# Five of the first eight modulation slabs summed on TensorE as rows instead of on VectorE as columns

## The reference, cut to what matters

```
mod = silu(c) @ ada_w + ada_b                 # c: 2048 values, ada_w: 2048 x 6144
shift, scale, gate = split(mod, 3)
h = rms_norm(x, norm_g) * (1 + scale) + shift
proj = h @ w_in                               # 2048 x 9296
```

## Time and profile before

| | us |
|---|---|
| median of 3 runs | 2428.26 (2428.01 to 2428.3) |
| the profiled execution: its time | 2428.43 |
| its span (first to last instruction) | 2426.6 |
| TensorE busy | 2384.8 (98%) |
| VectorE busy | 1973.3 (81%) |
| ScalarE busy | 1299.3 (54%) |
| GpSimd busy | 99.0 (4%) |
| HBM traffic | 212 GB/s over the span |

### The profile page before, as it was taken

One profiled execution on the slowest core, in us unless ns is written; L12 is line 12 of the kernel. 1 busy time (PEld: TensorE's weight loads), 2 busy tenths in 40 slices (PEclk: granted clock), 3 DMA queues, 4 the chain that ended last, 5 costly groups with the idle time before them and its releaser, 6 DMA issues.

```text
span 2426.6 us, 28811 instructions
## 1 busy us (share of the span) xinstructions
PE 2384.8 (98%) x11030; PEld 1979.5 (82%) x11030; DVE 1973.3 (81%) x2564; ACT 1299.3 (54%) x1703; POOL 99.0 (4%) x150
## 2 busy tenths in 40 slices
PE   5999999999999999999999999999999999999998
PEld 4888878888888888888888888888888888888887
DVE  6998988766889899897777768965699898988776
ACT  4757765445555555654444544554555555555443
POOL 0210000000000000000000212100000000000000
PEclk8999999999999999999999999999999999999999
DMA  9997665474566566566656655446666565565654
GB/s 383 360 385 246 240 208 171 166 262 167 192 208 208 191 208 196 186 199 215 229 188 205 196 196 193 160 142 203 218 210 200 188 212 188 195 222 189 224 191 156
DMA packets 190649, 515.46 MB, mean 212 GB/s; under 512 B 17920, under 2 KB 18208, under 8 KB 188208
## 3 DMA queue, kind: packets, MB, share of 16 engines
q1 hardware_dynamic: 178160, 465.31, 56.5%
q0 software_dynamic: 11824, 46.14, 5.1%
q10 hardware_dynamic: 528, 2.16, 0.2%
HBM read 507.26 MB, written 6.29 MB: 212 GB/s over the span
## 4 chain that ended last, share of the span: by engine, by line
PE 95%; DVE 2%; SPq 1%; DMA 0%; issue 0%; ACT 0%; DVEq 0%; ACTq 0%
PE acc L808 18%; PE acc L810 17%; PE acc L809 17%; PE acc L1276 4%; PE acc L1275 4%; PE acc L1277 4%; PE wk L1276 4%; PE wk L1275 4%; PE wk L1277 4%; PE acc L1317 1%; PE acc L1316 1%; PE acc L1318 1%; PE wk L1317 1%; PE wk L810 1%; PE wk L809 1%; PE wk L1316 1%
## 5 line engine op out<-in xcount | busy, mean ns | idle before, releaser
L2098 DVE TENSOR_TENSOR lo<-raw,hi 128x1024 fp32r<-128x1024 f32 (+2 forms) x428 | 486.8, 1188 | 110.2 <-ACT hi L1486 108.6
L1486 ACT ACTIVATE hi<-raw 128x1024 fp32r<-128x1024 f32 (+2 forms) x428 | 414.6, 1026 | 253.0 <-PE acc L810 122.1
L2100 DVE SCALAR_TENSOR_TENSOR lo<-raw,gcols,hi 128x1024 fp32r<-128x1024 f32 (+1 forms) x392 | 479.7, 1267 | 50.8 <-ACT hi L1486 48.3
L808 PE MATMUL acc<-hi,h 128*128 128x512 f32 x1312 | 519.4, 396 | 1.5 <-DVE lo L2098 0.5
L810 PE MATMUL acc<-hi,h 128*128 128x512 f32 x1312 | 511.7, 390 | 0.0
L809 PE MATMUL acc<-lo,h 128*128 128x512 f32 x1312 | 511.3, 390 | 0.0
L1486 ACT ACTIVATE hi<-raw,gcols 128x1024 fp32r<-128x1024 f32 (+1 forms) x392 | 416.6, 1124 | 140.4 <-PE acc L810 59.6
L808 PEld LDWEIGHTS acc<-hi,h 128*128 128x128 f32 x1312 | 246.8, 188 | 53.7 <-issue 2.7
L810 PEld LDWEIGHTS acc<-hi,h 128*128 128x128 f32 x1312 | 246.6, 188 | 52.3
L809 PEld LDWEIGHTS acc<-lo,h 128*128 128x128 f32 x1312 | 246.9, 188 | 49.1
L808 PE MATMUL acc<-hi,g_hi 128*128 128x512 f32 x544 | 211.9, 390 | 0.0
(11 more groups left out here) (445 smaller groups left out, 3403.8 us busy)
## 6 DMA issues: line engine op xcount, KB each, us to landing
raw<-in_w_ffn_gate SPq DMA_DIRECT2D x176, 512.0 KB, 3.8
raw<-in_w_ffn_up SPq DMA_DIRECT2D x176, 512.0 KB, 4.7
raw<-in_w_ffn_down SPq DMA_DIRECT2D x176, 512.0 KB, 4.7
raw<-in_w_in SPq DMA_DIRECT2D x144, 512.0 KB, 4.8
raw<-in_w_kv SPq DMA_DIRECT2D x64, 512.0 KB, 4.9
ada_raw<-in_ada_w POOLq DMA_DIRECT2D x38, 512.0 KB, 7.2
gate_raw<-in_ada_w POOLq DMA_DIRECT2D x32, 512.0 KB, 6.2
raw<-in_w_out SPq DMA_DIRECT2D x32, 512.0 KB, 4.8
```

Source lines behind the costliest of these rows:

```text
L808: pe.matmul(o, l_hi, w_hi[:, c], start=first, stop=False, skip_group_check=loaded)
L1486: ins = act.activation(hi[:, m % HI_SLOTS, c], raw[:, r, c], ACT.Copy, scale=scale)
L2098: ins = vec.tensor_tensor(lo[:, r, c], raw[:, r, c], hi[:, m % HI_SLOTS, c], ALU.subtract)
L2100: ins = vec.scalar_tensor_tensor(out=lo[:, r, c], in0=raw[:, r, c], scalar=gcols[:, st.gain, k:k + 1], in1=hi[:, m % HI_SLOTS, c], op0=ALU ...
```

## The change

Slabs 0, 1, 2, 3 and 5 are summed on TensorE, with the operands the other way round: a column of `silu(c)`, 128 partitions x 1, is stationary, and the slab is the moving operand, 512 columns at a time. Each slab takes four products of 128x512; all of them accumulate into one row of 2 x 512 sums in PSUM banks 2 and 3 (partition 0). ScalarE copies that row to SBUF (`ada_row`), and eight products with one row of 128 as stationary operand and a single 1.0 as moving one turn it into the eight PSUM columns, onto which `quarter_columns` adds what VectorE has summed. VectorE keeps slabs 4, 6 and 7 of the first eight. The transpose of the gains moves behind the first row sum; the row sum of slab 5 stands between `turn_xn` 1 and 2; the eight products stand between `turn_xn` 4 and 5; only `turn_xn` 6 and 7 are left behind `quarter_columns`. On SP the fetches of modulation slabs 11 and 12 move one `w_in` slab later, each with its wait.

```
-    PE_ADA = (1,)
+    PE_ADA = (0, 1, 2, 3, 5)
+    VEC_FIRST = (4, 8, 16, 24)
...
# SP
             if m == 3:
                 sp.wait_ge(xn_ready, 2)
                 ada_fetch(10, quarter_landed[2])
+            if m == 4:
                 sp.wait_ge(ada_added, added(7))
                 ada_fetch(11, early_landed[2])
-            if m == 4:
+            if m == 5:
                 sp.wait_ge(ada_added, added(8))
                 ada_fetch(12, early_landed[3])
...
# TensorE
-        pe.wait_ge(gains_in, 16 * 7)
-        pe.transpose(acc[:, 0, 0:P], rows[:], ident[:]).then_inc(rows_turned, 1)
...
+        def ada_row_sum(a):
+            ada_wait(pe, a)
+            for part in range(2):
+                for e in range(2):
+                    b = part * GW + e * HALF
+                    ins = pe.matmul(acc[0:1, 2 + e, :], c_col[:, 2 * a + part:2 * a + part + 1], ada_slot(a)[:, b:b + HALF],
+                                    start=a == PE_ADA[0] and part == 0, stop=a == PE_ADA[-1] and part == 1)
+            ins.then_inc(ada_taken, 1)
+
+        def row_into_columns():
+            pe.wait_ge(row_copied, 1)
+            pe.wait_ge(gains_out, 1)
+            for f in range(4):
+                for e in range(2):
+                    b = e * HALF + f * P
+                    pe.matmul(quarter_col(acc, e, f), ada_row[0:1, b:b + P], ones[0:1, 0:1], start=f % 2 == 0, stop=False,
+                              skip_group_check=True)
+
+        def turn_xn_when_parked(i):
+            if i >= 4:
+                pe.wait_ge(xn_parked, i - 3)
+            turn_xn(i).then_inc(turned, 1)
...
         pe.wait_ge(c_silu, 1)
+        ada_row_sum(0)
+        pe.wait_ge(gains_in, 16 * 7)
+        pe.transpose(acc[:, 0, 0:P], rows[:], ident[:]).then_inc(rows_turned, 1)
+        for a in (1, 2, 3):
+            ada_row_sum(a)
         pe.wait_ge(xn_ready, TT)
-        for i in range(4):
-            turn_xn(i).then_inc(turned, 1)
+        for i in range(2):
+            turn_xn_when_parked(i)
+        ada_row_sum(5)
+        for i in range(2, 5):
+            turn_xn_when_parked(i)
+        row_into_columns()
+        turn_xn_when_parked(5)
         quarter_columns(0, acc, False)
-        for i in range(4, 8):
-            pe.wait_ge(xn_parked, i - 3)
-            turn_xn(i).then_inc(turned, 1)
+        for i in range(6, 8):
+            turn_xn_when_parked(i)
...
# ScalarE
         conv_to(0)
-        for i in range(4):
+        for i in range(2):
+            park(i)
+        act.wait_ge(ada_taken, len(PE_ADA))
+        act.activation(ada_row[:].rearrange("p (e n) -> p e n", e=2), acc[0:1, 2:4, :], ACT.Copy).then_inc(row_copied, 1)
+        for i in range(2, 4):
             park(i)
...
# VectorE, in ada(a)
-                if k == 0 and a < N_MOD:
+                if kk == 0 and a in VEC_FIRST:
```

More of the change, by code:

```diff
@@ L156, in build @@
     ones_r = at("ones_r", [P, P], slot(1), F32R)
+    ada_row = at("ada_row", [1, GW], G0 + 79)
     ada_sum = [gate[:, 0:GW], gate[:, GW:D], tmp1, tmp2, gate[:, 0:GW], gate[:, GW:D]]
@@ L532, in build @@
     x_fetched = sem("x_fetched")
+    row_copied = sem("row_copied")
     own_landed = sem("own_landed")
@@ L945, in quarter_columns @@
                 ins.then_inc(ada_turned, 1)
-        pe.wait_ge(c_silu, 1)
[L948 to L957, removed]
```

## The result

| | before | after |
|---|---|---|
| median, us | 2428.3 (2427.85 to 2429.66, 9 runs) | 2433.28 (2431.42 to 2437.1, 9 runs) |
| ratio to before, 95% interval | | 1.002 (1.0011 to 1.0028) |
| span of the profiled execution, us | 2426.6 | 2431.5 |

The changed kernel is slower, by 5.0 us or 0.2%; the forecast was 3.4 us faster. The opening went as the prediction said or better. The loss is made 20 to 30 us behind it, in one wait and the slower clock that follows it.

A forecast was written before the change was run, and what follows sets the result against it. TensorE, busy 2384.8 of 2426.6 us, bounds the kernel; an earlier product start, worth 3.4 us by product 9, takes the profiled 2428.43 to 2425.0, or 2424.9 as median (that execution is 0.17 above it); range 2423.0 to 2429.0.

The forecast's parts named there:

- VectorE's sum 2.4 us earlier: Opening, VectorE: without slab 5, and with slab 6 waiting for its landing, its sum ends at 36.85 instead of 39.26.
- Row sums at 6.8 us for slab 0 and 3.5 to 3.7 from slab 1 on: Opening, TensorE: slab 0 summed at the lower clock, 1.2 GHz, later slabs at the upper, 2.4 GHz.
- never raised: Rival, opening: one-column row sums never raise TensorE's clock, everything behind is 11 to 12 us late; 2440, chance 0.12.
- TensorE late: Rival, opening: clock drops behind slab 5's sum, 2427.7; harder form, slab 5 itself at 1.2 GHz, 2430.9; chance 0.18.
- Eight small products done by 36.1, transpose 5 by 36.7: Opening, TensorE: both finish just before VectorE's sum; TensorE is free 0.15 us ahead of it.
- Columns at the lower level, start 3.7 us earlier: Opening: columns at 1.2 GHz, two transposes behind them instead of four; large products start at 42.3 instead of 46.05.
- all at the upper clock: Rival, opening: columns, transposes and first products also run at 2.4 GHz, products start at 41.3; 2423.8, chance 0.20.
- The first products gain what the start gains: Large products behind the opening: they keep the 3.7 us earlier start, with 2.3 us still at the lower clock.
- Scales of the second quarter at 85.5, product 9 gains 3.4: Second quarter: VectorE's tables end at 85.5 instead of 87.87, scales gain 3.5, product 9 behind them 3.4 us.
- The SP edit worth 0: SP's queue: moving modulation slabs 11 and 12 behind `w_in` 3 and 4 costs nothing, since VectorE adds them much later.
- For the landings of `w_in` behind the start I show no row; I take 0, with half a us of doubt: DMA landings of `w_in` after the products start: assumed to cost the earlier start 0, at most 0.5 us.
- nothing comes of it: Rival, 50 to 98 us: a `w_in` landing or ScalarE hand-over gives the gain back; 2428, chance 0.08.

The follow-up runs named there:

- e9: e2 with modulation slabs 16 and 17 also held on GpSimd until VectorE has summed slab 15: 2425.28 us, ratio 0.9987 to the kernel before.
- e5: The kernel before plus only the hold of two slab sums on GpSimd's slabs 13 to 15, no row sums: 2429.6 us, ratio 1.0006.
- e2: The changed kernel with GpSimd's fetches of slabs 13 to 15 waiting for two more VectorE slab sums: 2426.62 us, ratio 0.9992 to the kernel before.
- e3: The changed kernel with SP's order put back, slabs 11 and 12 not moved: 2433.36 us, ratio 1.002 to the kernel before.
- e1: The changed kernel with GpSimd's fetches of slabs 13 to 15 waiting for one more VectorE slab sum: 2429.57 us, ratio 1.0003 to the kernel before.
- e4: The changed kernel with ScalarE converting `w_in` slab 5 one product later, behind the bank hand-over: 2431.53 us, ratio 1.0013 to the kernel before.
- e6: The kernel before with only transposes 4 and 5 moved ahead of the columns, VectorE's sum untouched: 2427.75 us, ratio 0.9998.
- e10: e9 with GpSimd's small rows sent behind slab 14 instead of 15: 2429.17 us, ratio 1.0003 to the kernel before.

## Why the prediction was wrong, point by point

- **VectorE's sum 2.4 us earlier:** right. The columns started 39.31 - 36.93 = 2.4 earlier, behind `gate`.
- **Row sums at 6.8 us for slab 0 and 3.5 to 3.7 from slab 1 on:** right, 6.55 and 3.5 to 3.6. The rival *never raised* fell. *TensorE late* did not occur in this profile, but a part of its harder form did in e9, with the same opening: slab 5 took 5.29 instead of 3.59 (the rival had 6.8) and the columns started behind TensorE's own queue, at 38.18. So where the clock falls is in part luck of the execution, and that the forecast came close here is so too.
- **Eight small products done by 36.1, transpose 5 by 36.7:** right, 36.0 and 36.6.
- **Columns at the lower level, start 3.7 us earlier:** half right. The clock fell at 38.0, in the columns, so the first pair took 38.02 - 36.93 = 1.1 instead of 1.9 and the start gained 4.4. This is between the forecast and the rival *all at the upper clock*. The Trainium skill ("TensorE: Matmul & The Clock Gate", Part 4) says that transposes don't count as busy for the clock; here the clock fell 5.4 us behind the last row sum, over transposes and small products alike, so this trace does not tell the two apart. The opening of before speaks against the Trainium skill here. It has only the 16 transposes between 22.0 and 39.3 us; in e5, whose opening is the same, they took 3.54 us instead of 3.67, because the last ones ran faster, and the granted clock stayed at 1.00 behind them until 34.1. So there the clock rose over transposes alone; the difference is 0.13 us in one profile, and what makes it rise stays open.
- **The first products gain what the start gains:** 0.4 too much, since the lower level now reached 3.2 us into them.
- **Scales of the second quarter at 85.5, product 9 gains 3.4:** wrong for the changed kernel (93.83 and a loss of 4.8), right for the mechanism once the landing is in time: 85.31 in e2 and 86.47 in e9, and product 9 gains 2.7 and 2.6. The rest is the wait of product 8 in e2, 0.88, and the later start in e9.
- **The SP edit worth 0:** right in the time (e3, 2433.36 against 2433.28), but not because slab 12 is early enough: VectorE waited 3.48 us for it.
- **"For the landings of `w_in` behind the start I show no row; I take 0, with half a us of doubt":** this is the step that failed. The term is 6.9 us of wait and 1.8 of clock. I had costed the SP edit, but not the queue of GpSimd, which the change does not touch and whose fetches are released by VectorE, the engine that the change makes faster. The trace of before held it. `hi` 5 waited 2.97 us for its landing, the hand-over behind it began at 65.92 and its first bank was done at 66.5, and product 4 started at 69.00: 2.5 us of slack, less than the 3.7 by which I moved TensorE forward. With the start that came about, net 4.0 earlier (64.99), a delay of 1.6 us was due even at an unchanged landing (4.0 - 2.5, and 0.14 from the hand-over to the product); the later landing adds 5.4, and together they make the 7.0 by which product 4 missed its due start.
- **The rival *nothing comes of it*** named the place (a landing of `w_in`, or the hand-over on ScalarE) and had 0.08. Its price was wrong: it was capped at the gain. A delayed transfer is not bounded by the gain that set it off, and the clock adds to it. That is why the range ended 4.3 us short.
- **What the runs show and what stays open.** That GpSimd's earlier fetches cause the late landing, and with it most of the loss, is shown: landing and wait follow the hold (e1, e2), SP's order does not cause it (e3), ScalarE's order passes it on (e4), and moving TensorE without VectorE does not set it off (e6). The 1.6 us that were due without it are worked out from the rows, not run by themselves. e9 starts its products 3.3 us earlier than the kernel before, has 2.6 of it at product 9, 2.5 in the span and 3.0 in the median; what more slab 5 at the upper level would bring there was not separated. A split of the DMAs' time other than by the queues' turns was not tried.

## What to carry to other kernels

When a change makes an engine faster, list the transfers that this engine releases, on every queue, and ask whether the DMAs are full at that time; if they are, each of them moves ahead of something, and the slack of the landing that it delays belongs in the sum. Behind an opening that gains, hold back the fetches of what is not needed soon: here one wait raised by two rounds turned 5.0 us of loss into 1.7 us of gain, not clear of the noise, and two more slabs held made it 3.0, which is. Bound a rival of this kind by the bytes that change places divided by the rate that is left, not by the gain.

## What the runs showed of the hardware

- A stationary operand of a single column is enough for the upper clock. The one-column row sums of slab 0 ran at 0.82 us an instruction and those of slabs 1 to 3, from 15.30 on, at 0.44. The load of such a column took 84 ns.
- A transfer of 512 KB took 20.1 us from issue to landing at a total rate of 418 GB/s, where it took 10.7 in the kernel before at 416.
- Short packets take a queue's turn for few bytes. Between 65 and 70 us of after GpSimd's queue carries the small rows, in the view by queue:

```profile
q0 software_dynamic: 229, 0.40, 51.1%
q1 hardware_dynamic: 273, 0.98, 50.7%
```

  It moved 0.40 MB in 51% of the engines' time; between 60 and 65 us of before it had moved 1.10 MB in 53.9%. In e10 slab 15 stood behind these rows, and its two halves took 12.5 us from issue to landing (median) where they took 7.5 in e9.
- The clock fell 3.6 us into the 6.9 us wait and took 1.8 us more from the products behind it. This price does not follow the length of the wait. A product takes 5.44 us at the upper level; behind waits of 2.56 and 2.80 us (e3) it took 7.15 and 8.44, behind one of 3.47 (e1) 6.93, and behind one of 2.57 (e4) 5.57. In the first of these the clock fell only when the products were running again.
